# Per-token sums of squares on TensorE: one fp32 product, or two passes over a rounded part and its remainder

## What is computed

```python
def _rmsnorm(x, w):
    xf = x.astype(jnp.float32)
    y = xf * lax.rsqrt(jnp.mean(xf * xf, axis=-1, keepdims=True) + EPS)
    return (y * w.astype(jnp.float32)).astype(x.dtype)
...
    q = _rmsnorm(q, q_norm_w)   # (B, S, 8, 64)
    k = _rmsnorm(k, k_norm_w)   # (B, S, 2, 64)
```

## Time and profile before

| | |
|---|---|
| time, median of 3 runs | 2435.66 us (2435.24 to 2436.48) |
| time of the profiled execution | 2435.2 us |
| its span, from the first to the last instruction | 2433.6 us |
| PE busy | 2382.2 us, 98% of the span |
| DVE busy | 1412.4 us, 58% |
| ACT busy | 951.0 us, 39% |
| POOL busy | 147.2 us, 6% |
| mean granted TensorE clock | 0.999 |

### The profile page before, as it was taken

One profiled execution on the slowest core, in us unless ns is written; L12 is line 12 of the kernel. 1 busy time (PEld: TensorE's weight loads), 2 busy tenths in 40 slices (PEclk: granted clock), 3 DMA queues, 4 the chain that ended last, 5 costly groups with the idle time before them and its releaser, 6 DMA issues. The chain is left out here.

```text
span 2433.6 us, 36578 instructions
## 1 busy us (share of the span) xinstructions
PE 2382.2 (98%) x12718; PEld 1961.2 (81%) x12718; DVE 1412.4 (58%) x2096; ACT 951.0 (39%) x1697; POOL 147.2 (6%) x157
## 2 busy tenths in 40 slices
PE   5999999999999999999999999999999999999998
PEld 4888788888888878888888887888888888788886
DVE  6677663454668755245466866535556685643544
ACT  4466432223356633122335653212234664321222
POOL 0021000000003100000000300000000130000000
PEclk9999999999999999999999999999999999999999
DMA  4211222234321222224332122222432212222241
GB/s 148 97 63 54 96 95 95 95 111 144 104 92 53 71 95 96 95 95 140 111 104 87 53 79 93 97 95 95 142 119 94 78 45 96 92 99 95 95 146 70
DMA packets 63172, 232.63 MB, mean 96 GB/s; under 512 B 7361, under 2 KB 7361, under 8 KB 62401
## 3 DMA queue, kind: packets, MB, share of 16 engines
q1 hardware_dynamic: 55728, 202.64, 25.0%
q0 software_dynamic: 7312, 28.32, 3.3%
HBM read 222.54 MB, written 8.39 MB: 95 GB/s over the span
## 5 line engine op out<-in xcount | busy, mean ns | idle before, releaser
L1354 PE MATMUL ps<-h_h,w_h 128*128 128x512 f32 x2004 | 789.3, 394 | 16.0 <-DVE w_l L803 7.9
L1354 PE MATMUL ps<-h_h,w_l 128*128 128x512 f32 x2004 | 780.9, 390 | 0.0
L1354 PE MATMUL ps<-h_l,w_h 128*128 128x512 f32 x2004 | 780.8, 390 | 0.0
L803 DVE TENSOR_TENSOR w_l<-stage,w_h 128x1024 fp32r<-128x1024 f32 x381 | 466.7, 1225 | 274.5 <-ACT w_h L443 258.2
L443 ACT CAST w_h<-stage 128x1024 fp32r<-128x1024 f32 x381 | 398.5, 1046 | 552.1 <-PE ps L1354 543.9
L1354 PEld LDWEIGHTS ps<-h_h,w_h 128*128 128x128 f32 x2004 | 376.6, 188 | 111.6 <-DVE w_l L803 13.3
L1354 PEld LDWEIGHTS ps<-h_h,w_l 128*128 128x128 f32 x2004 | 376.6, 188 | 78.6
L1354 PEld LDWEIGHTS ps<-h_l,w_h 128*128 128x128 f32 x2004 | 376.9, 188 | 77.8 <-issue 1.9
L1354 PE MATMUL ps<-ff_h,w_h 128*128 128x512 f32 x1036 | 404.6, 391 | 0.0
L1354 PE MATMUL ps<-ff_h,w_l 128*128 128x512 f32 x1036 | 403.1, 389 | 0.0
L1354 PE MATMUL ps<-ff_l,w_h 128*128 128x512 f32 x1036 | 403.1, 389 | 0.0
(11 more groups left out here) (185 smaller groups left out, 1847.2 us busy)
## 6 DMA issues: line engine op xcount, KB each, us to landing
stage<-w SPq DMA_DIRECT2D x385, 512.0 KB, 3.3
x_next<-x POOLq DMA_DIRECT2D x20, 512.0 KB, 6.4
out<-xs POOLq DMA_DIRECT2D x32, 256.0 KB, 2.3
xs<-x POOLq DMA_DIRECT2D x8, 512.0 KB, 4.7
xs<-x POOLq DMA_DIRECT2D x4, 1024.0 KB, 5.4
bia<-bias POOLq DMA_DIRECT2D x1, 1024.0 KB, 5.0
cst<-con SPq DMA_DIRECT2D x1, 704.0 KB, 4.5
prm<-par SPq DMA_DIRECT2D x1, 39.5 KB, 1.9
```

The lines of the kernel that those rows point to most:

```text
L803: dve.tensor_tensor(w_l[:, b, 0:k], stage[:, s, 0:k], w_h[:, b, 0:k].bitcast(F32), ALU.subtract).then_inc(w_lo.sem, 1)
L1354: return pe.matmul(o, a, b, start=start, stop=stop)
```

## The change

The squares are also formed by ACT, as fp32r (`nq_h`). DVE's fp32 squares stay, and DVE takes the remainder `nq_l = nq - nq_h`, as fp32r. PE sums both parts into one PSUM bank with an fp32r copy of the constant, `k_half`. ACT makes that copy once, between the squares and the root of the first norm of the program. `nq_h` lies over `pts` and `ht`, `nq_l` over part of `ti`.

```diff
+            nq_l = sb("nq_l", [P, 2, TOK], F32R, s)
...
+        with ExitStack() as s:
+            sb("under_nq_h", [P, 2, 2, TOK], F32, s)
+            nq_h = sb("nq_h", [P, 2, TOK], F32R, s)
...
+        k_half = sb("k_half", [P, P], F32R)
...
# ACT, before the loop over groups
+            act.wait_ge(const_loaded, 16)
+            act.copy(k_half[:], cst[:, K_HALF, :]).then_inc(half_ready, 1)
             root(N1, 0)
...
# ACT, in a group
+                def norm_hi(n):
+
+                    if n == 1:
+                        act.wait_ge(nsum_done.sem, nsum_done.after(g, 0))
+                    act.wait_ge(copied.sem, copied.after(g, n + 2))
+                    act.nop(nofuse=True)
+                    act.activation(nq_h[:, n % 2], aq[:, n - 1] if n else akr[:], ACT.Square).then_inc(nsq_hi.sem, 1)
...
                 act.copy(akr[:], ps[:, A0, :]).then_inc(copied.sem, 1)
+                norm_hi(0)
...
                     act.copy(aq[:, j], ps[:, A0 + (U_AQ + j) % 2, :]).then_inc(copied.sem, 1)
+                    norm_hi(j + 1)
                     split_hi(g, CONV, U_AQ + 2 + j - CONV)
...
# DVE
                 def norm_square(n):
                     dve.wait_ge(copied.sem, copied.after(g, n + 2))
-                    dve.tensor_tensor(nq[:, n % 2], src(n), src(n), ALU.mult).then_inc(nsq_ready.sem, 1)
+                    dve.tensor_tensor(nq[:, n % 2], src(n), src(n), ALU.mult).then_inc(nsq_full.sem, 1)
+
+                def norm_low(n):
+                    own(nsq_full, g, n + 1)
+                    dve.wait_ge(nsq_hi.sem, nsq_hi.after(g, n + 1))
+                    dve.tensor_tensor(nq_l[:, n % 2], nq[:, n % 2], nq_h[:, n % 2].bitcast(F32),
+                                      ALU.subtract).then_inc(nsq_ready.sem, 1)
...
                 norm_square(0)
+                norm_low(0)
                 for j in range(PAIRS):
                     t = j
                     norm_square(j + 1)
+                    norm_low(j + 1)
                     split_lo(g, CONV, U_AQ + 2 + j - CONV)
...
# PE
+            pe.wait_ge(half_ready, 1)
             with pe.Fori(0, GROUPS) as g:
...
-                    mm(ps[:, NS, :], cst[:, K_HALF, :], nq[:, n % 2]).then_inc(nsum_done.sem, 1)
+                    mm(ps[:, NS, :], k_half[:], nq_h[:, n % 2], True, False)
+                    mm(ps[:, NS, :], k_half[:], nq_l[:, n % 2], False, True).then_inc(nsum_done.sem, 1)
```

More of the change, by code:

```diff
@@ L299, in build @@
         copied = signal("copied", 6)
+        half_ready = ctx.enter_context(nc.semaphore("half_ready"))
+        nsq_full = signal("nsq_full", NORMS)
+        nsq_hi = signal("nsq_hi", NORMS)
         nsq_ready = signal("nsq_ready", NORMS)
```

## The result

The change made the kernel slower: 2441.81 us, median of 13 runs, against 2436.38 us of the kernel before in 13 runs. The ratio is 1.0024, with a 95% interval of 1.0017 to 1.0031. The forecast was 2434.1 us, with a range of 2431.5 to 2438.0. Just as telling is the spread: the runs of the kernel before lie between 2434.24 and 2436.87 us, those of the changed kernel between 2437.58 and 2446.14. The profiled execution is the slowest of them (2446.14 us, span 2444.6 us, mean granted TensorE clock 0.993). Of the 13 executions none has a mean clock above 0.997, and the four at 0.997 are the four fastest (2437.6 to 2439.0 us).

The account below looks back on a forecast made before the run. PE, busy 98%, was taken as the bound, with an ACT-DVE-POOL chain level to within 0.80 us before the block stage. Four groups at -0.41 us gave -1.6: 2435.66 - 1.6 = 2434.1 us, range 2431.5 to 2438.0.

Parts of the forecast that it names:

- the clock rival: TensorE's clock falls in the new gap before the block stage, losing 2.4 us a group: about 2442 us, chance 0.08.
- What PE saves: In the norm sums, two fp32r passes of 0.46 us replace fp32 sums of 0.95 and 0.87: 2.37 us a group.
- What ACT's square costs: ACT's added square behind each copy of aq pushes back ACT's later work: 0.55 us each, between 0.51 and 0.65.
- How the chain and DVE's wait meet: The chain enters the block inverse 0.29 us late, DVE's 0.70 us wait there vanishes: -0.41 us a group, -1.6 in all.
- `norm_low` costs nothing: DVE's added remainder, 0.69 us per sum, is covered by DVE's wait for ACT's cast before split_lo.
- the edits at nothing: The first square, the k_half copy and the wait of norm_sum(4) fall into existing waits; uncovered, a few tenths a group.
- The rival of the free square: ACT's square is free and PE sets the pace: -2.17 us a group, 2427.0 us; chance of the full gain 0.08.

Follow-up runs that it names:

- after_b: The changed kernel unedited, run again on one chip beside its version with two filler matmuls: 2442.31 us, against 2436.43 of the kernel before.
- fill1: The changed kernel with one fp32 matmul that nobody reads in PE's gap before the block products: 2437.07 us, against 2436.70 of the kernel before.
- fill2: The changed kernel with two fp32 matmuls that nobody reads in PE's gap before the block products: 2437.16 us, against 2436.70 of the kernel before.
- fill2_b: The changed kernel with the same two unread matmuls, repeated on one chip beside the unedited changed kernel: 2436.38 us, against 2436.43 of the kernel before.
- hidden: The changed kernel with ACT's squares and DVE's remainders of norms 1 to 3 moved into idle time: 2432.58 us, against 2437.04 of the kernel before.
- hidden_fill: The changed kernel with those squares and remainders moved, plus one unread matmul before the block products: 2432.04 us, against 2437.04 of the kernel before.
- actdve_alone: The changed kernel with PE's old fp32 sum put back, ACT's squares and DVE's remainders made but unused: 2437.74 us, against 2436.70 of the kernel before.
- before: The kernel before the change, unedited: 2436.38 us beside the changed kernel's first runs.
- gap_half: The kernel before with 4 matmuls of unit Z+3 left out in each group: 2435.43 us, against 2436.43 of the kernel before.
- pe_alone: The kernel before with only PE's two fp32r passes, both over the same rounded squares: 2428.79 us, against 2436.70 of the kernel before.
- after: The changed kernel as first measured: 2441.81 us, against 2436.38 of the kernel before.
- after_again: The changed kernel unedited, once more on the chip of the runs with moved squares: 2443.64 us, against 2437.04 of the kernel before.
- gap_alone: The kernel before with 8 of 24 matmuls of unit Z+3 left out in each group: 2442.78 us, against 2437.04 of the kernel before.

## Why the prediction was wrong, by its own steps

**The step that failed** is the weighing of the clock rival. The forecast named it with its place (a gap from about 178.4 to 180.5 us), its rows and its price (about 2442 us; measured 2441.8), and gave it 0.08. Against it stood one row: PE had gone on at full speed after 1.93 us of idle time at 38.19 us. That row is one execution of something that changes from one execution to the next. The same gap, 1.92 to 1.94 us long, stands in front of the same full 128x512 matmuls in all 13 profiled executions of this document's kernels. In seven of them (`after_b`, `fill1`, `fill2`, `fill2_b`, `hidden`, `hidden_fill`, `actdve_alone`) the granted clock is at 0.50 behind it, for about 3.4 us each time. PE's timeline of `after_b`, and one window in that stretch:

```profile
38.30 0.79 PE L1382 MATMUL ps<-h_h,w_h 128*128 128x512 f32 x1 [1.93 <-DVE w_l L823]
38.89 0.63 PE L1382 MATMUL ps<-h_l,w_h 128*128 128x512 f32 x1
...
41.77 0.39 PE L1382 MATMUL ps<-h_h,w_l 128*128 128x512 f32 x1
42.00 0.40 PE L1382 MATMUL ps<-h_h,w_h 128*128 128x512 f32 x1
```

```profile
39.00:40.00 1.00, 1.00 (x4) 0.80 (x3) 1.00 (x2) 0.00 (x0) 0.00 (x0) 0.50 1.06 442
```

Nine starts take 42.00 - 38.30 = 3.70 us here, and 2.18 us in the profile of the changed kernel that has no such fall (38.25 to 40.43). So one costs about 1.5 us. The nine profiled executions without a fall in the block stage divide by it. The runs of each of these kernels lie at two levels, 1.5 to 2 us apart: the profiles of `before`, `gap_half` and `pe_alone`, without such a fall, stand at the lower, the other six at the upper. That PE went on at full speed at 38.19 us was luck, and no evidence against the rival.

In the four profiles with a gap of 1.76 to 1.86 us in front of the block products (`after`, `after_again`, `after_b`, `gap_alone`) the clock fell behind eight of the 16 gaps, about as often as behind the gap at the start. What differs is how long it stays down: 6.8 to 20.5 us in these eight, 3.4 us in those seven. Behind the gap of the block stage come small products of 64x32, scores, in most groups a second gap of up to 0.67 us, and more small products. That these draw a fall out fits all profiles, but no run changed them alone, so it stays argued. That the gap is needed is shown from both sides, by filling it and by making it in the kernel before. The rule of the Trainium skill, "TensorE: Matmul & The Clock Gate", section "Why this matters for your kernels", warned of idle gaps between bursts. The trace agrees that a gap can do it, after one of 1.8 us; the gaps of which the page warns are longer, and here the measurement decides.

The price of a fall was set at no more than 2.4 us a group for all four groups. Measured, two of four groups of the profiled execution fell, for 2.5 and 8.8 us: fewer falls, and a dearer one. That the rival's 2442 us met the median was partly luck.

**What PE saves**, 2.37 us a group forecast, was 1.73: `sc(0)` starts at 178.38 against 180.11 before. The two passes are 0.22 us apart, but the next fp32 matmul starts later than I let it:

```profile
131.51 0.39 PE L1382 MATMUL ps<-nq_h,k_half 128*128 128x512 f32 x1
131.73 0.40 PE L1382 MATMUL ps<-nq_l,k_half 128*128 128x512 f32 x1
132.06 1.16 PE L1382 MATMUL ps<-row,cst 64*128 64x128 f32 x8
```

A sum costs 132.06 - 131.51 = 0.55 us and not 0.46. I had set the step from fp32r to fp32 products at nothing. So the first four sums saved 0.40 us each and not 0.49, and the fifth 0.34 and not 0.41 (1.10 to 0.76 us from its start to the second matmul of the unit behind it), 1.94 us in all. The other 0.2 us are not traced.

**What ACT's square costs**, h, was taken as 0.55 us with an upper bound of 0.65, and each copy was let overlap `pack` by 0.10 us. In the trace the square starts 0.68 us after the copy, not 0.60, and the cast 1.22 us after it, where it was 0.60. So h is 0.62, and the copies don't overlap `pack`. The copies 1 to 3 came at +0.45, +0.30 and +0.13 us against before, where +0.27, +0.02 and -0.26 were forecast. The chain entered the block inverse at 163.65 instead of 162.93, +0.72 us, where +0.29 was forecast and +0.99 was the bound:

```profile
132.55 0.59 ACT L633 COPY aq<-ps 128x512 f32<-128x512 f32 x1
133.23 0.63 ACT L542 ACTIVATE nq_h<-aq 128x512 fp32r<-128x512 f32 x1
133.77 1.03 ACT L451 CAST w_h<-stage 128x1024 fp32r<-128x1024 f32 x1
```

**How the chain and DVE's wait meet** was right in kind. The wait of 0.70 us inside the block inverse is gone, but not all of its 0.70 us is won: the reduction before it ends at 170.03 + 0.29 = 170.32 and `split_lo` starts at 170.44. This step of 0.12 us the sum had at nothing, and it is there in `pe_alone` too (168.51 to 168.63). `split_lo` starts 0.13 us later than before, instead of 0.41 earlier. Of these 0.54 us, 0.43 are the later entry and the rest is this step. POOL's copies begin 0.14 us later:

```profile
163.65 0.70 DVE L1045 STREAM_TRANSPOSE tmp<-xi 128x512 f32<-128x512 f32 x1
...
170.03 0.29 DVE L1115 TENSOR_REDUCE tb<-tmp 128x32 f32<-128x128 f32 x1
170.44 1.23 DVE L823 TENSOR_TENSOR w_l<-stage,w_h 128x1024 fp32r<-128x1024 f32 x1
...
177.35 0.71 DVE L1067 STREAM_TRANSPOSE pts<-ss 128x512 f32<-128x512 f32 x1
```

```profile
178.21 5.73 POOL L412 COPY xi<-pts 32x512 f32<-32x512 f32 x4 [11.92 <-DVE pts L1067]
```

They take 0.2 us less, which I can't explain and which brings `update(0, 0)` to 184.03 against 184.10. So without a fall in the block stage the change is worth nothing: `fill2_b` is at 0.9999 of the kernel before (-0.05 us by the medians), where -1.6 us was forecast with bounds of -2.4 and +1.2.

**`norm_low` costs nothing** and the edits at nothing held: DVE still waits 0.17 us for the cast behind it.

**The rival of the free square** (2427.0 us) gave nearly the right time for a kernel in which it is free: PE's part alone ran at 2428.8 us, with most of the squares moved into idle time 2432.6 us.

## What to carry to other kernels

Sparing the busiest engine some work only moves it into a wait when another chain is level with it. Before such a change, trace that chain back and ask whether it can follow, and put added instructions into the idle time of their engine, not in front of its next task: here this order was worth 11 us. A new gap on TensorE is not free even where nothing waits on it: when the runs spread more than before and their mean clock is lower, look at the granted clock in windows behind the new gap, and prove it by filling the gap with work that nobody needs. Don't take one gap of one execution without a fall as a sign that such a gap is harmless: here the same gap at the start of the program was followed by a fall in seven of 13 profiles.

## What the runs showed of the hardware

The granted clock fell to 0.50 after gaps of only 1.76 to 1.86 us (each followed by small products, mostly with a second gap of up to 0.67 us among them), in eight of 16 such places of four profiled executions, and not in others with the same timeline to within 0.05 us. It stayed low for 6.8 us in five of them, 10.2 us in two and 20.5 us in one, while PE was busy nearly without a break by its records. After a gap of 1.92 to 1.94 us in front of full 128x512 matmuls it fell in seven of 13 profiled executions and stayed low for 3.4 us each time. With the gap before the block products at 0.9 us the falls were rare, and with it filled no run showed their times.
